# Gate pre-activations of an mLSTM mixer: gate weights as the moving operand, or as the standing one with two turns

## Reference

```python
def split_proj(u, w_in):                     # w_in: (1024, columns); 16 of the columns are the gates
    return jnp.split(u @ w_in, np.cumsum(SPLIT_SIZES)[:-1].tolist(), axis=-1)

def mlstm_prepare(p, gate_b):
    ...
    g = (p[3] + gate_b).astype(jnp.float32).reshape(b, t, 4, NH_M).transpose(2, 0, 3, 1)
    return q, k, v, g

def mlstm_direction(q, k, v, i_pre, f_pre, state, reverse):
    logf = jax.nn.log_sigmoid(f_pre)
    ...

def mlstm_chunkwise(q, k, v, i_pre, logf, state):
    ...
        bcum = jnp.cumsum(fc, axis=-1)
        log_d = jnp.where(causal, bcum[..., :, None] - bcum[..., None, :] + ic[..., None, :], -jnp.inf)
    ...
```

## Time and profile before

| | us |
|---|---|
| median of 3 runs | 2310.88 |
| lowest, highest | 2310.04, 2311.03 |
| the profiled execution, its own time | 2308.48 |
| its span in the trace | 2306.7 |
| PE busy | 2256.7 (98%) |
| DVE busy | 767.0 (33%) |
| ACT busy | 431.8 (19%) |
| granted TensorE clock, mean | 0.998 |
| bytes moved, mean rate | 639.71 MB, 277 GB/s |

### The profile page before, as it was taken

How to read it: one execution, slowest core, us unless ns; L and a number is a source line. 1 busy time by engine, 2 the same in 40 slices (tenths; PEclk the granted TensorE clock), 3 DMA queues, 4 the chain that set the end, 5 groups by cost and what they waited for, 6 DMA issues and landing times.

```text
span 2306.7 us, 31507 instructions
## 1 busy us (share of the span) xinstructions
PE 2256.7 (98%) x12894; PEld 1708.7 (74%) x12894; DVE 767.0 (33%) x1866; ACT 431.8 (19%) x1031; POOL 43.6 (2%) x66
## 2 busy tenths in 40 slices
PE   8999999999999999999999999999999999999998
PEld 7888888888898888888887885555555555555555
DVE  7944342433053441210646632222222211111212
ACT  3542210201033211110135121111111111111112
POOL 0600000000000000000000000000000000000000
PEclk9999999999999999999999999999999999999999
DMA  9644446568424444336522659999999999999997
GB/s 391 231 146 146 147 178 240 215 226 308 182 92 157 156 162 146 128 127 230 155 91 92 260 214 395 426 426 428 428 428 429 427 427 427 429 428 427 426 427 294
DMA packets 65976, 639.71 MB, mean 277 GB/s; under 512 B 7464, under 2 KB 9896, under 8 KB 12624
## 3 DMA queue, kind: packets, MB, share of 16 engines
q1 hardware_dynamic: 65872, 638.25, 69.8%
HBM read 630.86 MB, written 4.21 MB: 275 GB/s over the span
## 4 chain that ended last, share of the span: by engine, by line
PE 81%; DMA 15%; DVE 2%; issue 1%; ACT 0%; SPq 0%; DVEq 0%
PE bank L704 29%; PE bank L1306 15%; DMA arena<-in_experts 10%; PE bank L701 6%; PE bank L806 5%; DMA ring<-in_experts 4%; PE bank L1343 4%; PE bank L691 3%; PE bank L718 3%; PE bank L935 2%; PE bank L1297 2%; PE bank L1265 1%; PE bank L817 1%; PE bank L1253 1%; PE bank L764 1%
## 5 line engine op out<-in xcount | busy, mean ns | idle before, releaser
L704 PE MATMUL bank<-arena,ring 128*128 128x256 f32 x3136 | 680.3, 379 | 0.0
L704 PEld LDWEIGHTS bank<-arena,ring 128*128 128x128 f32 x3136 | 595.4, 190 | 80.7
L2462 DVE TENSOR_SCALAR arena<-bank 128x256 f32<-128x256 f32 x64 | 27.2, 425 | 672.0 <-PE bank L1306 672.0
L1306 PE MATMUL bank<-arena 128*64 128x256 f32 x2048 | 231.3, 380 | 12.6 <-DMA arena<-in_experts 12.6
L1306 PE MATMUL bank<-ring,arena 128*64 128x256 f32 x2048 | 234.1, 383 | 6.0 <-DMA ring<-in_experts 6.0
L1306 PEld LDWEIGHTS bank<-ring,arena 128*64 128x64 f32 x2048 | 143.3, 137 | 111.0 <-issue 29.5
L1306 PEld LDWEIGHTS bank<-arena 128*64 128x64 f32 x2048 | 144.5, 137 | 101.0 <-DMA arena<-in_experts 20.6
L701 PE MATMUL bank<-ring,arena 128*128 128x256 f32 x608 | 132.0, 379 | 0.0
L701 PEld LDWEIGHTS bank<-ring,arena 128*128 128x128 f32 x608 | 115.4, 190 | 15.6
L1759 ACT ACTIVATE arena<-arena 128x256 f32<-128x256 f32 x64 | 26.7, 416 | 531.3 <-DVE arena L2462 531.3
L806 PE MATMUL bank<-arena,ring 128*128 128x256 f32 x576 | 124.6, 379 | 0.0
(11 more groups left out here) (325 smaller groups left out, 2105.6 us busy)
## 6 DMA issues: line engine op xcount, KB each, us to landing
ring<-in_dense SPq DMA_DIRECT2D x203, 1024.0 KB, 4.9
arena<-in_experts SPq DMA_DIRECT2D x96, 2048.0 KB, 31.2
ring<-in_experts SPq DMA_DIRECT2D x87, 2048.0 KB, 30.9
ring<-in_experts SPq DMA_DIRECT2D x16, 1024.0 KB, 32.8
arena<-park SPq DMA_DIRECT2D x3, 1024.0 KB, 7.0
arena<-in_dense SPq DMA_DIRECT2D x2, 1024.0 KB, 19.3
park<-ring SPq DMA_DIRECT2D x2, 1024.0 KB, 8.1
ring<-arena SPq DMA_DIRECT2D x16, 128.0 KB, 5.7
```

Of the source, the lines that this page charges most:

```text
L704: ins = nc.tensor.matmul(o, w[:, k, j * P:(j + 1) * P], src[:, k, :], start=(k == 0), stop=(k == KT - 1))
L1306: ins = nc.tensor.matmul(o, XGT[:, k, e * CAP:(e + 1) * CAP], w[:, k, :], start=False, stop=(k == KT - 1), skip_group_check=True)
```

## The change

The two operands of the gate product change places. The 16 gate weights of a chunk stand, and all 256 tokens of the chunk move, so that one product serves both halves of the tokens: `gate_rows` makes 8 products per unit (only in half j = 0) where `gate_columns` made 16. The result is 16 rows of 256 tokens. ScalarE copies it to SBUF (`rows_out`, `GROWS`), and one unit later TensorE turns it with two transposes (`gates_turned`) back to 128 tokens by 16 gates, where ScalarE (context) and VectorE (stream) read it as before. `gates` counts to 4 now.

```diff
+        GROWS = TMP[0:16, 768:1024]
...
-            def gate_columns(t, k, tokens):
-
-                return nc.tensor.matmul(banks[WORK + 1][:, 384 + 16 * t:400 + 16 * t], tokens, GW[:, k, :],
+            def gate_rows(k, src):
+
+                return nc.tensor.matmul(banks[WORK + 1][0:16, 0:T], GW[:, k, :], src[:, k, :],
                                         start=(k == 0), stop=(k == KT - 1), skip_group_check=True)
+
+            def gates_turned(rows):
+
+                pe.wait_ge(sem(rows + "_done_by_act"), before(rows + "_done_by_act") + 1)
+                for t in range(2):
+                    ins = nc.tensor.transpose(banks[WORK + 1][:, 384 + 16 * t:400 + 16 * t], GROWS[:, t * P:(t + 1) * P],
+                                              ident[0:16, 0:16])
+                ins.then_inc(sem("gates"), 1)
...
-                            if n == 0:
-                                gate = gate_columns(j, k, UC[:, k, j * P:(j + 1) * P])
+                            if n == 0 and j == 0:
+                                gate = gate_rows(k, UC)
...
             for n in range(6):
                 early(n)
+                if n == 1:
+                    gates_turned("ctx_rows")
...
-                        tokens = H[:, k, j * P:(j + 1) * P]
-                        ins = nc.tensor.matmul(half_of(u, j), tokens, w[:, k, :], start=(k == 0), stop=(k == KT - 1))
-                        gate = gate_columns(2 + j, k, tokens)
+                        ins = nc.tensor.matmul(half_of(u, j), H[:, k, j * P:(j + 1) * P], w[:, k, :],
+                                               start=(k == 0), stop=(k == KT - 1))
+                        if j == 0:
+                            gate = gate_rows(k, H)
...
             first_values()
-            stage("mv", H, token_major=True, first=1, count=2)
+            stage("mv", H, token_major=True, first=1, count=1)
+            gates_turned("gate_rows")
+            stage("mv", H, token_major=True, first=2, count=1)
             pe.wait_ge(sem("gate_steps"), 2)
...
+            def rows_out(name, gates):
+
+                act.wait_ge(sem("gates"), gates)
+                nc.scalar.copy(GROWS, banks[WORK + 1][0:16, 0:T]).then_inc(sem(name + "_done_by_act"), 1)
...
                 if n == 0:
-                    act.wait_ge(sem("gates"), 1)
+                    rows_out("ctx_rows", 1)
+                if n == 1:
+                    act.wait_ge(sem("gates"), 2)
                     nc.scalar.copy(GC, tiles(banks[WORK + 1][:, 384:416], 2)).then_inc(sem("ctx_gates"), 1)
...
-            take(0, 8)
+            take(0, 7)
+            rows_out("gate_rows", 3)
+            take(7, 8)
...
-            dve.wait_ge(sem("gates"), 2)
-            me(V.tensor_tensor(GT[:, 2:4, :], tiles(banks[WORK + 1][:, 416:448], 2), gate_b, ALU.add))
+            dve.wait_ge(sem("gates"), 4)
+            me(V.tensor_tensor(GT[:, 2:4, :], tiles(banks[WORK + 1][:, 384:416], 2), gate_b, ALU.add))
```

More of the change, by code:

```diff
@@ L208, in build @@
                 ("acc", KT, ["ffn0", "ffn1"]), ("out_slab", FT // 2, ["ffn0", "ffn1"]),
-                ("done_by_act", 1, ["silu_ctx", "silu_c", "lam_exp", "f_exp", "f_ln"]),
+                ("done_by_act", 1, ["silu_ctx", "ctx_rows", "silu_c", "lam_exp", "gate_rows", "f_exp", "f_ln"]),
                 *((f"{i}_in", 32, ["ada_place", "rows_of_head"]) for i in range(4))):
```

## The result

The changed kernel takes 2315.57 us (median of 11 runs, 2312.9 to 2317.4), the kernel before 2310.04 us beside it (11 runs, 2308.26 to 2311.03). The ratio is 1.0024 [1.0017, 1.0032]: slower by 5.5 us, where 5.8 were forecast. The profiled execution of the changed kernel took 2315.76 us. Of all executions behind this document one, of e10_packed_ctx, took 7062.22 us at a mean granted clock of 0.315; it is left out of that kernel's figures, and nothing here shows what held it up.

The account below looks back on a forecast made before the run. PE was taken to bound the kernel, the later expert-weight stream moving with it. Two gated units at +4.56 us and turns at +1.22 gave +5.8 us, a median from 2310.88 to 2316.7 us, range 2313.6 to 2319.4.

Parts of the forecast that it names:

- The pace of the passes: Gate products in both changed units: 3.45 us a unit by passes against 3.57, a win of 0.12 us a unit.
- The round trip: Each gate product between whole-array products: changing the array's shape and back costs 0.30 us, 2.4 us a unit.
- the first rival: Gate products and transposes: no price for the change of shape, +0.2 us, 2311.1 us; little or no price: chance 0.11.
- A unit, +2.28 us: Each unit with gates, context and stream: 12.76 us against 10.48, +4.56 us for both.
- The turn, 0.61 us: Two transposes after each gated unit: 0.22 us plus 0.39 for the shape change, 1.2 us in all.
- No added wait: PE at turns and cumulative sums: copy done about 2.9 us early, VectorE's chain 3.1 us early, so no wait.
- The second rival: PE reaches the cumulative sums before VectorE's chain is through; a chain 7 us longer gives 2320.7 us; chance 0.03.
- What they gain or lose counts in full: Changed units at 65 to 75 and 1010 to 1020 us lie on PE's chain; their change reaches the end whole.
- The profiled execution: Whole kernel's profiled run: from 2308.48 to 2314.3 us.
- The rival in which the swap pays: Gate products packed four to a slot: 6.9 us a unit becomes 1.7, -5 us, 2305.9 us; chance 0.02.

Follow-up runs that it names:

- e10_packed_ctx: Kernel before, with gate products packed four side by side on column groups at the context unit alone: 2310.11 us, ratio 1.0004.
- e1_wide80: Changed kernel with 80 columns standing in each gate product instead of 16, so it has the whole array: 2310.70 us, ratio 1.0004.
- e3_grouped: Changed kernel with a unit's eight gate products in a row between the unit's two halves: 2311.17 us, ratio 1.0006.
- e4_split: Changed kernel with the stream's two transposes apart, one amid the second values unit, one behind it: 2315.66 us, one run.
- e5_late_turn: Changed kernel with the stream's turn one unit later, right ahead of the cumulative sums: 2322.13 us, ratio 1.0050.
- e6: Changed kernel with the context unit put back as before, only the stream's unit changed: 2312.66 us, ratio 1.0013.
- e8_packed_again: Repeat, for time alone, of the changed kernel with gate products packed four side by side in both units: 2308.82 us, ratio 0.9999.
- e7_packed: Changed kernel with gate products in a row, four side by side on column groups, turned by a selection-matrix product: 2307.51 us, ratio 0.9996.
- e9_packed_stream: Kernel before, with packed gate products at the stream's unit alone and the selection matrix made behind the convolution: 2308.15 us, ratio 0.9994.

## Why the prediction was right, and what in it was not

**The pace of the passes** (-0.12 us a unit): right. In e1_wide80 the period is 0.863 us, and within the group of e3_grouped 16 narrow passes take as long as 16 wide ones.

**The round trip, 0.30 us for each gate product**: right, and it carries the result. 0.301 us measured, where the traces of before gave 0.34 and 0.39 for larger pieces and 0 for line 1022. The choice between these was the forecast. e1_wide80 and e3_grouped show it by taking the changes of shape away with all other work left in place. They also settle the first rival for these products: few standing columns do not make the way free, since 16 pay 0.30 us where the 8 of rows 5 pay nothing. That rows 5 are free because their instruction words select all column groups fits this, but no run varied the words alone. The closeness is luck in part: the 0.30 was worked out from the 0.05 us between two places of which one cuts the rows and the other the columns, and it came out to 0.001 us. The Trainium skill, "TensorEngine Tiling (Array Packing)", section Key Properties (a change of tiling mode drains the TensorE), agrees with both runs.

**A unit, +2.28 us**: measured 2.30. **The turn, 0.61 us**: this term was mis-sized; it measured 0.41. I had added 0.39 us for the change of shape, from the differential attention, and 0.11 for each transpose. e4_split splits it otherwise: 0.36 for the change and the first transpose of 16 columns together, 0.05 for the next. The sum is 5.4 us by the rows in place of 5.8.

**No added wait**: right, with 2.7 and 3.1 us to spare where 2.9 and 3.1 were forecast. The second rival's wait exists one unit later (e5_late_turn), and I had priced such a wait too low, at its own length: the clock that falls behind it adds 2.7 us to 3.9.

**"What they gain or lose counts in full"**: right for the loss: in the trace it is 2.7 us ahead of the join and 2.6 us behind it. For a gain at the context unit it does not hold in general: VectorE's convolution was through 0.4 us before PE came in the profile of before, and later than PE in those of e6, e8 and e10. I had read PE as on the chain without a break from the first units on, and had not asked how close the next engine was.

**The profiled execution**: forecast at 2314.3 us, came at 2315.76, because PE's start was 1.84 us later in it. The counts from the context unit on do not have that (5.36 us).

**The rival in which the swap pays**: its condition was rightly excluded for this program, since all eight products go to the same columns. Its mechanism is real in e7_packed, at 3.9 us in the trace where the rival had 5: it left out the round trip (0.34 us a unit) and took 0.2 us for a turn of 0.45. The Trainium skill, the same page, section Performance Considerations, recommends this form with fourfold column tiling; the rows agree on the products, and the median shows how much of that reaches the end here.

**Open.** Some executions of e7 and e8 are near 2312 us with a mean clock of 0.994 to 0.995, where the others have 0.996 to 0.999. No trace of such an execution was taken. A fall of the clock after the wait at 128 us could explain them, but it is not shown, and two traces speak against it: in e10_packed_ctx the granted clock is 1.00 in every stretch of 2 us from 124 to 134 us, across a wait of 3.25 us, and in e8_packed_again from 124 to 136 us, across 1.89 us. The clock also fell where PE had not waited at all. In e9_packed_stream, just ahead of the experts, after 1.00 from 1364 to 1366 us:

```profile
1366.00:1368.00 2.00, 2.00 (x12) 2.00 (x12) 0.99 (x7) 1.31 (x4) 0.00 (x0) 0.53 1.07 459
1368.00:1370.00 2.00, 2.00 (x13) 2.00 (x12) 1.36 (x9) 1.82 (x3) 0.00 (x0) 0.62 0.98 418
```

PE is busy throughout, and this execution loses 1.56 us between 1346 and 1746 us against the kernel before (399.62 against 398.06). e4_split has such a dip too, at 1374 us, and e5_late_turn from 1382 to 1386 us (0.54 and 0.61); there it is 1.5 us of the 8.1 by which its trace is longer than the changed kernel's from the first context unit on. The kernel before, e7, e10 and the changed kernel do not have it in their traces. Its cause is open, and it is one source of the spread of some us between executions. And none of the packed kernels is faster than the kernel before beyond its interval.

## What to carry to other kernels

A narrow product between products of the whole array pays for the change of the array's shape, here 0.30 us against 0.43 us for the product itself, whatever its own passes save. Group such products, pad their standing side until the program gives them the whole array, or put four side by side on groups of columns of their own; only the last was shorter in the traces than what stood here before, and no median shows it beyond its interval. And before a gain on the path is counted, look how near the next engine's work is, in more than one execution: with 0.4 us of room or none, 1.9 us of gain reached the join in one of three traces, while a loss at the same place counted in full.

## What the runs showed that I had not expected

After a pause of 3.9 us PE's granted clock stood at 0.50 for more than 4 us of full work and cost 2.7 us beyond the pause.

A wider standing operand was faster: 80 columns 0.863 us a period, 16 columns 1.164, 48 columns 1.191.

Float32 products with 32 standing columns, each on its own group of columns, ran four at a time: 16 passes of 256 columns in 0.86 us, four slots, and 0.34 us for the round trip.

The granted clock stood at 0.53 from 1366 to 1368 us in e9_packed_stream, with PE busy without a gap before and after, and at 1.00 across a wait of 3.25 us in e10_packed_ctx.

The first context unit starts between 64.12 us (e3_grouped) and 67.45 us (e5_late_turn) in the profiled executions (nothing is changed ahead of it in these two), as much as two thirds of the effect that was measured. A single pair of profiles would have given 7.2 us for the change in place of 5.4.
